# One hybrid two-block layer on one core: the norm's variance summed on VectorE, the inverse's last parts moved, the gates' chain one tile later

## The reference, cut to what matters

```
h    = rmsnorm(x)                                    # first norm, "n1"
q,k,v= silu(conv5(h @ w_in[q,k,v]))                  # 24 tiles of 128 channels, "t"
beta = sigmoid(b_raw);  g = -exp(A_log)*softplus(a_raw + dt_bias)     # gates
L    = strict(beta * k k^T * decay);  u,w = solve(I + L, ...)         # per chunk of tokens
S_t  = S*exp(g_last) + k_dec^T v_new                 # serial over chunks, both directions
...
u  = causal_conv31(a_val * sigmoid(a_glu))           # second block, even mixer
ya = silu(layernorm(u)) * silu(a_gate)               # layernorm: mean, then variance, "va"
y  = concat([ya, yb]) @ w_out
```

## Time and profile before

| | us |
|---|---|
| median of 3 runs | 1828.39 (1827.64 to 1830.2) |
| profiled execution, its own time | 1829.92 |
| its span, first to last instruction | 1828.1 |
| TensorE busy | 1747.4 (96% of the span) |
| VectorE / ScalarE / GpSimd busy | 824.5 / 679.7 / 861.4 |
| mean granted TensorE clock | 0.975 of full |

### The profile page before, as it was taken

The page is one execution under the profiler, slowest core; times in us unless marked ns, Lnnn a source line. Parts: engine busy times, 40 slices in busy tenths (PEclk is TensorE's granted clock), DMA queues, the critical chain, the costliest instruction groups (busy, mean ns, idle before and its releaser), DMA issues.

```text
span 1828.1 us, 22823 instructions
## 1 busy us (share of the span) xinstructions
PE 1747.4 (96%) x9151; PEld 1473.5 (81%) x9151; DVE 824.5 (45%) x1323; ACT 679.7 (37%) x997; POOL 861.4 (47%) x482
## 2 busy tenths in 40 slices
PE   7899869999999999999999999989999999999987
PEld 7888869998988888877888878868887788877766
DVE  7668925923323301122111121127999842457642
ACT  5656523332332222233222232233233443365651
POOL 3356423232334644544555554445477645456552
PEclk9899969999999999999999999989999989999998
DMA  5475258463422324222222223322222312222222
GB/s 193 136 226 164 70 155 254 133 173 110 145 70 71 96 98 140 92 93 92 93 93 92 93 92 104 104 70 93 94 98 89 112 58 93 92 93 92 93 74 76
DMA packets 120145, 201.41 MB, mean 110 GB/s; under 512 B 32448, under 2 KB 71512, under 8 KB 120040
## 3 DMA queue, kind: packets, MB, share of 16 engines
q1 hardware_dynamic: 118552, 197.47, 34.3%
q10 hardware_dynamic: 1488, 2.48, 0.4%
HBM read 170.46 MB, written 29.46 MB: 109 GB/s over the span
## 4 chain that ended last, share of the span: by engine, by line
PE 85%; DVE 9%; ACT 3%; issue 2%; DMA 1%; POOL 1%; SPq 0%; DVEq 0%; ACTq 0%
PE ps L401 67%; PE ps L1733 3%; DVE cacc L2148 2%; PE ps L875 2%; PE ps L921 1%; PE ps L928 1%; PE ps L907 1%; PE ps L885 1%; PE ps L915 1%; PE ps L883 1%; PE ps L932 1%; PE ps L893 1%; DVE inv L615 1%; DVE ps L1341 1%; PE ps L1680 1%
## 5 line engine op out<-in xcount | busy, mean ns | idle before, releaser
L389 POOL TENSOR_TENSOR w_lo<-w_raw,w_hi 128x1024 fp32r<-128x1024 f32 x264 | 632.8, 2406 | 567.0 <-ACT w_hi L383 566.9
L401 PE MATMUL ps<-hp_hi,w_hi 128*128 128x512 f32 (+2 forms) x1664 | 558.2, 363 | 7.3 <-DVE cacc L2148 6.1
L401 PE MATMUL ps<-hp_lo,w_hi 128*128 128x512 f32 (+2 forms) x1664 | 553.3, 360 | 0.0
L401 PE MATMUL ps<-hp_hi,w_lo 128*128 128x512 f32 (+2 forms) x1664 | 553.2, 360 | 0.0
L401 PEld LDWEIGHTS ps<-hp_hi,w_hi 128*128 128x128 f32 x1664 | 297.7, 191 | 63.2 <-issue 7.5
L401 PEld LDWEIGHTS ps<-hp_lo,w_hi 128*128 128x128 f32 x1664 | 297.1, 190 | 50.3 <-issue 1.7
L401 PEld LDWEIGHTS ps<-hp_hi,w_lo 128*128 128x128 f32 x1664 | 297.4, 190 | 48.0
L383 ACT ACTIVATE w_hi<-w_raw 128x1024 fp32r<-128x1024 f32 x264 | 277.5, 1053 | 152.0 <-DMA w_raw<-in_w 144.3
L1221 DVE SCALAR_TENSOR_TENSOR ps<-u_in,par,ps 128x511 f32<-128x511 f32 (+14 forms) x240 | 176.7, 739 | 8.4 <-ACT ps L1213 0.8
L2148 DVE SCALAR_TENSOR_TENSOR cacc<-ps,par,cacc 128x528 f32<-128x528 f32 x96 | 73.6, 767 | 37.3 <-ACT cacc L1783 34.6
L2524 POOL TENSOR_TENSOR y_lo<-tmp,y_hi 128x512 fp32r<-128x512 f32 x22 | 28.4, 1289 | 105.6 <-ACT y_hi L1932 105.6
(11 more groups left out here) (397 smaller groups left out, 2575.5 us busy)
## 6 DMA issues: line engine op xcount, KB each, us to landing
w_raw<-in_w SPq DMA_DIRECT2D x264, 512.0 KB, 3.5
d_y<-zero SPq DMA_DIRECT2D x6, 688.0 KB, 6.1
d_x<-zero SPq DMA_DIRECT2D x6, 688.0 KB, 5.9
d_at<-at SPq DMA_DIRECT2D x16, 256.0 KB, 3.0
d_kc<-kc SPq DMA_DIRECT2D x16, 256.0 KB, 3.2
d_qd<-eg SPq DMA_DIRECT2D x16, 256.0 KB, 3.1
d_p<-dec SPq DMA_DIRECT2D x16, 256.0 KB, 3.4
AT<-d_at SPq DMA_DIRECT2D x16, 256.0 KB, 6.1
```

Of the source, the lines that this page charges most:

```text
L389: e.tensor_tensor(w_lo[:, u % RAW, :], w_raw[:, u % RAW, :], w_hi[:, u % RAW, :].bitcast(F32), ALU.subtract).then_inc(s_lo, 1)
L401: mm = e.matmul(ov, w, r[:, k, t0:t1], start=(first and n == 0 and p3 == 0), stop=(last and n == len(tiles) - 1 and p3 == 2))
```

## The change

Three edits.

The norm of the second block: square 0 goes to PSUM bank 6, the others to `row(1..7)`; DVE subtracts the mean first, then adds the squares one after another in bank 6, the last sum going to `row(7)`; PE sums this one row over partitions with four calls (`pe_cols`) at the end of `mixb` tile 1, and spreads the result at the end of tile 2, into bank 4. The rescaling of `x` and the additions of `mixb` tiles come later on DVE.

The first norm adds in PSUM from its first sum on. The tap and the scaling of tile 3 move ahead of the gates' first task, and `bat`, `gda`, `gdb`, `dk` each move one tile later.

`sub` 6 and 7 move from tiles 22 and 23 to tile 21, ahead of the convs of tiles 22 and 23. `pk(4)` and ACT's part of `pg(4)` move to the beginning of the change of hands.

```diff
-SIDE = {1: [("ba", 0)], 2: [("bat", 0)], 3: [("gda", 0)], 4: [("kt", 0), ("gdb", 0)], 5: [("kt", 1), ("dk", 0)],
-        6: [("ktm", 0), ("ks", 0)], 7: [("pg", 0), ("n2", 0)], ...
+SIDE = {1: [("ba", 0)], 3: [("bat", 0)], 4: [("kt", 0), ("gda", 0)], 5: [("kt", 1), ("gdb", 0)],
+        6: [("ktm", 0), ("ks", 0), ("dk", 0)], 7: [("pg", 0), ("n2", 0)], ...
-        20: [("vt", 1), ("sub", 4), ("msub", 3)], 21: [("vtm", 1), ("sub", 5), ("mw", 0)],
-        22: [("vt", 2), ("msa", 0), ("sub", 6)], 23: [("vtm", 2), ("msb", 0), ("sub", 7)],
+        20: [("vt", 1), ("sub", 4), ("msub", 3)], 21: [("vtm", 1), ("sub", 5), ("mw", 0), ("sub", 6), ("sub", 7)],
+        22: [("vt", 2), ("msa", 0)], 23: [("vtm", 2), ("msb", 0)],
...
# pe_program
             pe_msa(e, 1)
+            pe_pk(e, 4)
             pe_yx(e, 0, 0)
...
                 pe_ks(e, s, k)
-                if q == 0:
-                    pe_pk(e, 4)
...
+                if j == 1:
+                    e.wait_ge(*ad.at("va", KT - 1))
+                    pe_cols(e, row(7), 0).then_inc(ss.sem, 1)
                 if j == 2:
-                    e.wait_ge(*x0.at("x0", KT))
-                    for k in range(KT):
-                        e.wait_ge(*sq.at("va", k + 1))
-                        for c in range(NCH):
-                            mm = e.matmul(ps[:, 5, c:c + 1], row(k)[:, c * P:(c + 1) * P], cmat("mean1024")[:, 0:1],
-                                          start=k == 0 and c == 0, stop=k == KT - 1 and c == NCH - 1)
-                    mm.then_inc(ss.sem, 1)
                     e.wait_ge(*rc.at("va", 1))
-                    pe_spread(e, 5, 28).then_inc(tb_.sem, 1)
+                    pe_spread(e, 4, 28).then_inc(tb_.sem, 1)
...
# act_program
-                e.activation(sqv[:, k, :], x_in[:, k, :], ACT.Square).then_inc(sq.sem, 1)
+                e.activation(pair(sqv[:, k, :]) if k else ps[:, 6:8, 0:HALF], pair(x_in[:, k, :]), ACT.Square).then_inc(sq.sem, 1)
...
+                    if n != 3:
+                        act_tap(n)
                     if n == 2:
                         for k in range(3, KT):
                             first_hi(k)
+                        act_tap(3)
...
+            act_pg(e, 4)
             act_tc(e, 0, 0, 32)
             act_msa(e, 1)
             act_xc(e, 0, 0)
             act_msb(e, 1)
-            act_pg(e, 4)
...
-                e.activation(row(k), uc[:, k, :], ACT.Square).then_inc(sq.sem, 1)
+                e.activation(row(k) if k else ps[:, 6, :], uc[:, k, :], ACT.Square).then_inc(sq.sem, 1)
...
# dve_program
-                s = pair(sqv[:, 0, :]) if k == 1 else ps[:, 6:8, 0:HALF]
-                e.tensor_tensor(pair(cacc[:, 0, :]) if k == KT - 1 else ps[:, 6:8, 0:HALF], s, pair(sqv[:, k, :]), ALU.add).then_inc(ad.sem, 1)
+                e.tensor_tensor(pair(cacc[:, 0, :]) if k == KT - 1 else ps[:, 6:8, 0:HALF], ps[:, 6:8, 0:HALF], pair(sqv[:, k, :]), ALU.add).then_inc(ad.sem, 1)
...
                 if n == 2:
                     for k in range(4, KT):
                         first_row(k)
+                    scaled(3)
...
             dve_yc32(e, 0, 0)
+            dve_pk(e, 4)
...
                 dve_r(e, s, k)
-                if q == 0:
-                    dve_pk(e, 4)
...
+            e.wait_ge(*ss.at("mu", KT))
+            for k in range(KT):
+                e.tensor_tensor(uc[:, k, :], uc[:, k, :], ps[:, 4, :], ALU.subtract).then_inc(ln.sem, 1)
+            for k in range(1, KT):
+                e.wait_ge(*sq.at("va", k + 1))
+                if k > 1:
+                    e.wait_ge(*ad.at("va", k - 1))
+                e.tensor_tensor(row(7) if k == KT - 1 else ps[:, 6, :], ps[:, 6, :], row(k), ALU.add).then_inc(ad.sem, 1)
```

More of the change, by code:

```diff
@@ L1765, in first_hi, with act_tap @@
                 e.activation(h_hi[:, k, :], hf0[:, k, :], ACT.Copy).then_inc(hi.sem, 1)
+            def act_tap(n):
+                what, h = TILES[n]
+                b = 2 * (n % 2)
+                e.wait_ge(*(fd.at("n1", (1, 2, 4, 5)[n]) if n < 4 else (s_pe, n + 1)))
+                if n >= 2:
+                    e.wait_ge(*si.at("t", n - 1))
+                e.activation(pair(cacc[:, n % 2, :]), ps[:, b:b + 2, 0:HALF], ACT.Copy, scale=pcol(QKV[what][0], h)).then_inc(m_tap.sem, 1)
             for n in range(len(TILES) + 2):
@@ L1775, in act_program @@
                 if n < len(TILES):
[L1776 to L1782, removed]
-                    e.activation(pair(cacc[:, n % 2, :]), ps[:, b:b + 2, 0:HALF], ACT.Copy, scale=pcol(QKV[what][0], h)).then_inc(m_tap.sem, 1)
+                    if n == 2:
+                        for k in range(3):
+                            first_hi(k)
+                    if n != 3:
+                        act_tap(n)
                     if n == 2:
@@ L2014, in act_program @@
                 e.wait_ge(*ln.at("c", k + 1))
-                e.activation(row(k), uc[:, k, :], ACT.Square).then_inc(sq.sem, 1)
+                e.activation(row(k) if k else ps[:, 6, :], uc[:, k, :], ACT.Square).then_inc(sq.sem, 1)
             round_unit(e, BASE["mixb"] + 4)
             e.wait_ge(*ss.at("va", 1))
-            e.activation(small[:, 28:32], ps[:, 5, 0:4], ACT.Sqrt, bias=eps5_col).then_inc(rt.sem, 1)
+            e.activation(small[:, 28:32], ps[:, 4, 0:4], ACT.Sqrt, bias=eps5_col).then_inc(rt.sem, 1)
             round_unit(e, BASE["mixb"] + 5)
@@ L2139, in dve_program @@
                     acc, b = pair(cacc[:, n % 2, :]), 2 * (n % 2)
-                    if n in (2, 3):
-                        scaled(n)
-                        if n == 2:
-                            first_row(3)
+                    if n == 2:
+                        scaled(2)
+                        first_row(3)
                     e.wait_ge(*m_tap.at(n))
@@ L2385, in dve_program @@
                 e.scalar_tensor_tensor(x[:, k, :], x[:, k, :], pcol("fin1", k), ps[:, 5, :], ALU.mult, ALU.mult).then_inc(x0.sem, 1)
-            e.wait_ge(*ss.at("mu", KT))
-            for k in range(KT):
-                e.tensor_tensor(uc[:, k, :], uc[:, k, :], ps[:, 4, :], ALU.subtract).then_inc(ln.sem, 1)
-            for j in range(3):
-                add_b(j)
             e.wait_ge(*rt.at("va", 1))
             e.reciprocal(small[:, 28:32], small[:, 28:32]).then_inc(rc.sem, 1)
+            add_b(0)
+            add_b(1)
             e.wait_ge(*tb_.at("va", 1))
@@ L2396, in dve_program @@
                 if k < KT:
-                    e.tensor_tensor(uc[:, k, :], uc[:, k, :], ps[:, 5, :], ALU.mult).then_inc(ln.sem, 1)
+                    e.tensor_tensor(uc[:, k, :], uc[:, k, :], ps[:, 4, :], ALU.mult).then_inc(ln.sem, 1)
                 if k >= 1:
@@ L2400, in dve_program @@
                     e.tensor_tensor(row(k - 1), ps[:, 6 + (k - 1) % 2, :], sg_a[:, k - 1, :], ALU.mult).then_inc(la.sem, 1)
-                if k == 4:
-                    add_b(3)
+                if k in (1, 4):
+                    add_b(2 + k // 4)
             for j in range(4, KT):
```

2 lines of the change are left out of this document (1 added, 1 removed), and 2 rows, old and new, of the table SIDE.

## The result

The changed kernel takes 1800.43 us (median of 4 runs, 1799.39 to 1803.19), the kernel before 1828.04 in the same comparison: 27.6 us less, ratio 0.9846, interval 0.9835 to 0.9857. The forecast was 1802.7. The profiled execution took 1801.38 us, its span is 1799.6 us, the mean clock 0.982 instead of 0.975. PE is busy for 1732.0 us, 15 less than before, DVE for 827.7.

The account below looks back on a forecast made before the run. PE, busy 1747.4 of 1828.1 us, was taken as the bound, with losses in few places. Gains 11.3 + 3.5 + 10.9 = 25.7 us off 1829.92 gave 1804.2, less 1.5 for the median: 1802.7; own range 1799 to 1806, overall 1793 to 1811.

Parts of the forecast that it names:

- The norm, 11.3 us: Second block's norm: PE's 13.2 us of small products and low clock shrink to 1.9; 11.3 us gained, bounds 9 and 11.8.
- Rival 3: Second block's norm: DVE's additions take 1.97 us each, PE waits 6.7 us after tile 1; 1809.4 us, chance 0.05.
- First norm and gates, 3.5 us: Early stretch to tile 7: that tile starts 5.5 us ahead, taken as 3.5 for possible losses; bounds 5.5 and 1.3.
- The first norm's 1.2 us: First norm: with square 0 in PSUM all additions take 0.8 us, so PE begins its sum 1.2 us earlier.
- Rival 4: Gates' chain: stall and low clock both hit tile 7, and again before the inverse, no gain; 1806.2 us, chance 0.08.
- Inverse, 10.9 us: Inverse and change of hands: `pe_w` 8.2 us ahead, plus 2.65 from no second clock drop; 10.9 us, bounds 5 and 18.
- The scatter's 5.7 us: Inverse: the scatter, issued at 227.61 before, starts at 221.9 behind SP's last weight load, 5.7 us ahead.
- it rose 14.7 us after the first product: Change of hands: clock return after slot 0's first product, taken unchanged from the trace of before, at 254.8 us there.
- rival 1: Change of hands: clock returns early, after 4.8 us, until DVE's chain binds; 4.5 us more gain, 1798 us, chance 0.17.
- the terms of DVE's chain: Change of hands: state copied at 13.6 us, `dve_pk(4)` 3.7, `dve_r` and `dve_yc64` 1.1; ready at 19, needed at 18.4.
- Rival 2: Inverse: scatter not the lever, first product's start stays near 240 us, 5 us fall away; 1807.7 us, chance 0.14.
- Rival 5: Chain of slots: low clock stays after the pause from 222 us, 0.5 us per us; 1830 and more, chance 0.02.

Follow-up runs that it names:

- late_sum: Changed kernel with DVE's eight rescalings of x ahead of the seven additions of squares in the second block's norm; 1808.38 us.
- n1_only: Kernel before with only the first norm's change, its first square going to PSUM; 1827.91 us, ratio 0.9992.
- gates_only: Kernel before with only the gates' chain one tile later and tile 3's tap and scaling moved ahead; 1826.28 us, ratio 0.9982.
- inv_only: Kernel before with only the inverses' last two parts one unit earlier and the fifth pair's work ahead of slot 0; 1820.19 us, ratio 0.9946.
- sub_only: Kernel before with only the inverses' last two parts (`sub` 6 and 7) moved to tile 21; 1823.85 us, ratio 0.9971.
- norm_only: Kernel before with only the second block's norm changed, its variance summed on DVE; 1818.59 us, ratio 0.9936.
- warm_best: Changed kernel with unused PE products in nine waits, counts fitted to the trace of warm_fit; 1793.30 us, ratio 0.9802.
- warm_one: Changed kernel with 20 unused PE products in the wait ahead of the first inversion product; 1799.11 us, ratio 0.9837.
- warm_fit: Changed kernel with 88 unused PE products in nine waits, about half the counts of warm_all; 1798.66 us, ratio 0.9831.
- pk_only: Kernel before with only the fifth pair's work on PE, ACT and DVE ahead of the inversion steps; 1823.68 us, ratio 0.9966.
- warm_all: Changed kernel with 178 unused PE products in nine waits, lasting 41 us where the waits had 23; 1802.74 us, ratio 0.9853.
- before_warm: Kernel before with unused PE products in the two waits around the inversion's start, 54 and 15; 1824.85 us, ratio 0.9977.

## Why the prediction was right

**The norm, 11.3 us: right**, in the sum and in each step: eight instructions in 0.95 us, a spread of 1.05, the sum with 1.6 us to spare (1.4 forecast), 11.5 in the trace and 11.3 alone. late_sum shows the cover is real and thin. Rival 3, additions at 1.97 us, falls: they took 0.8.

**First norm and gates, 3.5 us: 5.4 measured**, inside its bounds of 1.3 to 5.5. The positions forecast without the deduction (tile 7 at 72.6) were right to 0.1 us. The deduction was for a stall of `gda` by POOL, which did not come (it ran from 61.33 to 63.0), and for the low clock. The first norm's 1.2 us were 0.7 in the changed kernel and 0.8 in n1_only; gates_only shows the clock taking 1.6 us of the gates when the low stretch lies on tile 7. Rival 4 is that, but not in full.

**Inverse, 10.9 us: 13.0 measured.** The scatter's 5.7 us were exact: SP's last weight load ends at 216.13, DVE's copy at 216.45, the scatter is issued at 216.53. The first product came 4.5 us early, not 5.1: the meeting with the load in the queues, priced at 0.6 without a row, took 1.2, if it is that. The mis-sized term is the clock behind it: "it rose 14.7 us after the first product" was read from one execution, and it rose after 8.8. inv_only, with this edit alone, shows the same forecast the other way: 16.4 us, 19.6 from first product to `pe_w` where the forecast's positions give 19.3, and an own lead of 10.4. So the mechanism held in both, and the size of this part varies by some 3 us with the clock's return, which the prediction had only as rival 1. A slip in it: the terms of DVE's chain, 13.6, 3.7 and 1.1, add up to 18.4 us and not to 19; PE waited 0.82 us for it, so the sign "no wait of DVE's at `pe_w`" was met only nearly. Rival 1 had the direction, with 4.8 us and 4.5 more gain; 2.2 more came. Rival 2 (scatter not the lever) falls by sub_only. Rival 5 falls: no low stretch of the changed kernel is longer than before's.

By the Trainium skill (TensorE: Matmul & The Clock Gate, section What's actually happening) the fast clock returns after one busy stretch. The changed kernel's trace agrees at 208 to 212 us, where it took 3.4 us, and not here: 8.8 us of back-to-back products in the changed kernel, 14.7 before.

**What was not in the sum:** the dip at 553 us, -1.7 us, with PE busy. The sum of 25.7 against 28.5 between the profiled executions is 5.4 + 13.0 + 11.5 + 0.3 - 1.7 = 28.5 (gates +1.9, inverse +2.1, norm +0.2, pieces +0.3, dip -1.7). The parts alone were 4.5 us above the forecast in this execution; that the whole came within 2.3 us of the forecast median is in part luck, since the dip took back 1.7.

What stays open: what decides in which kernel or execution the dips between 515 and 570 us come (none before, in norm_only, gates_only, n1_only, sub_only and warm_best; one in the changed kernel, warm_one and late_sum; two in inv_only and warm_fit; three in pk_only, warm_all and before_warm), and why the clock needs between 7.9 and 16.4 us of products to come back after the first product of slot 0. Each of these values is from one profiled execution.

## What to carry to other kernels

Price a wait of PE's not by its length but with the work behind it at half speed: 3.6 us of wait cost 6.6 here, and filling the two waits around the inversion with unused products won 9.0 us locally without moving a single result, of which 3.9 were left at the end. Where such a wait can't be removed, fill it to its end but not over it, with the instruction's own measured time: warm_fit with too few products kept a low stretch of 13.7 us, warm_all with too many gave the gain back. When a sum moves from PE to an idle engine, its place in that engine's queue decides, so look which of its neighbours PE doesn't need yet.

## What the runs showed of the hardware

A product of 128 columns in fp32 shows as two instructions of 0.115 us each at 2.4 GHz. The length of one wait of PE's does not tell whether the 1.2 GHz level follows: it followed 1.89 us (changed kernel, 20.4 us), 1.95 us (warm_fit, 230.2 us) and 2.69 us (warm_best, 163.3 us), and did not follow 2.38 us (gates_only, 61.9 us) or 2.62 us (warm_fit, 161.5 us). Products of one column did not hold the level up: before, from 1492 to 1502 us, PE was busy for 9.4 of 10 us and the clock was 0.59. And the level drops with PE busy throughout (4.00 of 4.00 us at 0.57 in inv_only), for stretches that cost 1.7 us, at places that differ between kernels whose program there is the same.
